# Seven half-block products for the down projections of two feed-forward parts, in an fp32 transformer kernel

## The reference, cut to what matters

```python
def swiglu_ffn(x, w_up, w_down):
    gate, up = jnp.split(x @ w_up, 2, axis=-1)
    return (jax.nn.silu(gate) * up) @ w_down
...
h = h + swiglu_ffn(rmsnorm(h, norm_ffn[l]), ffn_w_up[l], ffn_w_down[l])
```

## Time and profile before

| | |
|---|---|
| time, median of 3 runs | 1587.54 us (1587.21 to 1591.04) |
| span of the profiled execution | 1588.5 us |
| TensorE busy | 1557.8 us, 98% of the span |
| VectorE / ScalarE / GpSimd busy | 66% / 51% / 51% |
| TensorE's granted clock, mean | 0.995 of full speed |

### The profile page before, as it was taken

How to read it: one execution, slowest core, us unless ns; L and a number is a source line. 1 busy time by engine, 2 the same in 40 slices (tenths; PEclk the granted TensorE clock), 3 DMA queues, 4 the chain that set the end, 5 groups by cost and what they waited for, 6 DMA issues and landing times.

```text
span 1588.5 us, 26988 instructions
## 1 busy us (share of the span) xinstructions
PE 1557.8 (98%) x10227; PEld 1356.5 (85%) x10227; DVE 1050.6 (66%) x1622; ACT 816.2 (51%) x1334; POOL 812.8 (51%) x459
## 2 busy tenths in 40 slices
PE   6999999999999999999999999999999999999997
PEld 4888888888887878478998998988788998998996
DVE  6887587597597859977734643664666762572555
ACT  4555455355356535376633542654666652453453
POOL 1444345345345439827655654654116665564653
PEclk8999999999999999999999999999999999999999
DMA  9322322322323365712332332352112333233231
GB/s 376 140 93 80 120 83 91 119 82 90 119 81 102 128 116 153 187 53 81 107 119 80 106 119 81 105 182 96 54 41 68 106 112 100 93 106 115 85 117 69
DMA packets 53640, 172.86 MB, mean 109 GB/s; under 512 B 5403, under 2 KB 11580, under 8 KB 53052
## 3 DMA queue, kind: packets, MB, share of 16 engines
q1 hardware_dynamic: 47296, 159.90, 30.6%
q10 hardware_dynamic: 6268, 11.95, 3.2%
HBM read 165.48 MB, written 6.36 MB: 108 GB/s over the span
## 4 chain that ended last, share of the span: by engine, by line
PE 79%; DVE 3%; issue 2%; ACT 2%; POOL 2%; DVEq 0%; ACTq 0%; POOLq 0%
PE gps L2026 13%; PE gps L2028 12%; PE gps L2027 12%; PE gps L2449 6%; PE gps L2451 6%; PE gps L2450 6%; PE aps L2449 3%; PE aps L2451 3%; PE aps L2450 3%; PE gps L2386 2%; PE gps L2084 1%; PE gps L2086 1%; PE gps L2085 1%; POOL w_lo L619 1%; PE aps L2527 1%
## 5 line engine op out<-in xcount | busy, mean ns | idle before, releaser
L619 POOL TENSOR_TENSOR w_lo<-w_raw,w_hi 128x1024 fp32r<-128x1024 f32 x172 | 437.4, 2547 | 545.9 <-ACT w_hi L741 545.8
L2026 PE MATMUL gps<-xa_hi,w_hi 128*128 128x512 f32 x767 | 306.6, 400 | 2.6 <-DVE xa_lo L1380 2.6
L2027 PE MATMUL gps<-xa_lo,w_hi 128*128 128x512 f32 x767 | 299.9, 391 | 0.0
L2028 PE MATMUL gps<-xa_hi,w_lo 128*128 128x512 f32 x767 | 299.8, 391 | 0.0
L741 ACT CAST w_hi<-w_raw 128x1024 fp32r<-128x1024 f32 x172 | 180.0, 1046 | 155.6 <-PE gps L2028 75.2
L2026 PEld LDWEIGHTS gps<-xa_hi,w_hi 128*128 128x128 f32 x767 | 144.6, 188 | 35.3 <-DVE xa_lo L1380 4.1
L2028 PEld LDWEIGHTS gps<-xa_hi,w_lo 128*128 128x128 f32 x767 | 144.6, 188 | 31.1
L2027 PEld LDWEIGHTS gps<-xa_lo,w_hi 128*128 128x128 f32 x767 | 144.8, 189 | 27.6
L2026 PE MATMUL gps<-xb_hi,w_hi 128*128 128x512 f32 x378 | 148.2, 392 | 0.0
L2028 PE MATMUL gps<-xb_hi,w_lo 128*128 128x512 f32 x378 | 147.2, 389 | 0.0
L2027 PE MATMUL gps<-xb_lo,w_hi 128*128 128x512 f32 x378 | 147.1, 389 | 0.0
(11 more groups left out here) (428 smaller groups left out, 4324.9 us busy)
## 6 DMA issues: line engine op xcount, KB each, us to landing
w_raw<-weights_dram SPq DMA_DIRECT2D x268, 512.0 KB, 3.5
ada_w<-ada_in_dram SPq DMA_DIRECT2D x8, 1024.0 KB, 18.1
gates<-ret_tab_dram ACTq DMA_DIRECT2D x4, 1024.0 KB, 6.0
spread<-glu_scratch_dram SPq DMA_DIRECT2D x12, 270.0 KB, 5.1
rel_scratch_dram<-rel_rows ACTq DMA_DIRECT2D x1, 3072.0 KB, 34.5
x<-x_turned_dram SPq DMA_DIRECT2D x2, 1024.0 KB, 7.2
res<-xT_dram ACTq DMA_DIRECT2D x1, 2048.0 KB, 9.5
bias<-rel_scratch_dram ACTq DMA_DIRECT2D x1, 2048.0 KB, 9.8
```

The costliest lines, as they stand in the source:

```text
L619: TT(w_lo[:, j, :], w_raw[:, j, :], w_hi[:, j, :].bitcast(F32), ALU.subtract).then_inc(lo_ready[j], 1)
L2026: mm(gps[:, j, :], w_hi[:, j, w], x[0][:, k, :], start=k == 0, stop=False)
L2027: mm(gps[:, j, :], w_hi[:, j, w], x[1][:, k, :], start=False, stop=False)
L2028: last = mm(gps[:, j, :], w_lo[:, j, w], x[0][:, k, :], start=False, stop=k == blocks - 1)
```

## The change

The down projections of parts 0 and 1 of each layer become seven-product groups too, in one order with the up groups (`FF_ORDER`, 30 groups a layer: 22 up, 8 down). A down group makes two output chunks from the 8 hidden chunks of its part. Part 2 stays dense. The up group `("up", part + 1, 0)` is run ahead of the down groups of the part before it.

For this the hidden rows have to be mixed as the inputs were: after each odd hidden chunk VectorE makes three differences of 256 columns (a fourth, `t1`, is made after the even chunk), ScalarE casts the four together (`hidden_mix_high`), and VectorE makes their low parts (`hidden_mix_low`). The gated rows now go to SBUF (`hbuf`) rather than back to PSUM. The norm's factor is left off the up rows of these parts and applied to the results of the down groups (`down_added`), which are then added to `res`. TensorE waits for all mixed rows of a part ahead of its first down group. Weights are reordered on the host; their number is the same, 68 chunks a layer.

```diff
 FF_PARTS = (8, 8, 6)
+MIXED_PARTS = 2
...
+def ff_order():
...
+    order, starts = [], [sum(FF_PARTS[:part]) for part in range(len(FF_PARTS))]
+    for part, n in enumerate(FF_PARTS):
+        order += [("up", part, k) for k in range(1 if part else 0, n)]
+        if part < MIXED_PARTS:
+            order += [("up", part + 1, 0)] + [("down", part, m) for m in range(KC // 2)]
+    return order, starts
...
+                def silu(I, s):
                     act.wait_ge(evicted[s], I + 2)
                     nc.scalar.activation(sq[:, s, :], sq[:, s, :], ACT.Silu).then_inc(silu_ready, 1)
...
-                def hidden_high(f, k, s):
-                    act.wait_ge(ff_ready, f + 1)
-                    nc.scalar.copy(halves(hidden[:, k, :]), UP_ROWS[s]).then_inc(ff_hi, 1)
...
+                def hidden_high(f, part, k):
+                    row = hbuf[:, 2 * (k % 2), :]
+                    act.wait_ge(rows_free, f + 3)
+                    if part >= MIXED_PARTS:
+                        ins = nc.scalar.copy(hidden[:, k, :], row)
+                    elif k % 2 == 0:
+                        ins = nc.scalar.copy(hid_single(k // 2)[:, 0, :], row[:, 0:TH])
+                    else:
+                        ins = nc.scalar.copy(hid_double(k // 2)[:, :, 0, :], halves(row))
+                    ins.then_inc(hid_high, 1)
+                def hidden_mix_high(part, m):
+                    act.wait_ge(hid_mixed, mixes_before(layer, part) + m + 1)
+                    nc.scalar.copy(hid_mix(layer, m, 0), hid_rows).then_inc(hid_mix_high, 1)
...
+                for n in range(FF_PAIRS):
...
+                    kind, part, k = FF_ORDER[n - 1] if n else (None, None, None)
+                    early = kind == "up" and k == 0 and part > 0
...
+                    if more:
+                        first_row_high(I1, s1)
...
+                    if kind == "up":
+                        silu(up + (n - 1) // 2, 1 - s)
+                    if n > 1:
+                        first_copy(f, I, s)
+                    if more and n > 0:
+                        sums_high(I1, f + 1, s1)
+                    copied(f, 2, hbuf[:, 2 * s + 1, TH:], UP_SUM[s])
+                    if kind == "up" and not early:
+                        hidden_high(f - 1, part, k)
+                    copied(f, 3, hbuf[:, 2 * s + 1, 0:TH], UP_ROW[s])
...
+                    copied(f, 4, GATE_ROW[s][:, TH:], UP_ROW[s])
+                    if more:
+                        last_sum_high(f + 1, s1)
...
+                    if kind == "down" and k == KC // 2 - 1:
+                        act.wait_ge(tile_done[2 * (1 - s) + 1], up + (n - 1) // 2 + 2)
+                        hidden_high(f0 + FF_ORDER.index(("up", part + 1, 0)), part + 1, 0)
+                    if kind == "up" and part < MIXED_PARTS and k % 2 == 1:
+                        hidden_mix_high(part, k // 2)
...
             def ffn(layer, hidden_hi, hidden_lo, norm, n_next, build=None):
...
+                def gate_and_up(n, part, k):
+                    f, I, s = f0 + n, up + n // 2, n % 2
+                    if n == 0:
                         dve.wait_ge(rstd_ready, norm + 1)
                     dve.wait_ge(tile_done[2 * s + 1], I + 2)
                     TT(sq[:, s, :], GATE_ROW[s], rstd[:], ALU.mult).then_inc(evicted[s], 1)
                     own.done(TT(UP_ROWS[s], UP_ROWS[s], halves(hbuf[:, 2 * s + 1, :]), ALU.add))
-                    own.done(TT(UP_ROWS[s], UP_ROWS[s], halves(rstd[:]), ALU.mult))
-                    dve.wait_ge(silu_ready, f + 1)
-                    TT(UP_ROWS[s], UP_ROWS[s], halves(sq[:, s, :]), ALU.mult).then_inc(ff_ready, 1)
-                def hidden_low(f, k, s):
-                    dve.wait_ge(ff_hi, f + 1)
-                    TT(halves(hidden_lo[:, k, :]), UP_ROWS[s], halves(hidden_hi[:, k, :]).bitcast(F32), ALU.subtract).then_inc(ff_lo, 1)
-                    if s == 1:
-                        for j in (2, 3):
-                            dve.sem_inc(evicted[j], 1)
...
-                    for k in range(n):
-                        f, I, s = f0 + k, up + k // 2, k % 2
-                        if k > 0:
-                            gate_and_up(f - 1, up + (k - 1) // 2, 1 - s)
-                        if part == 0 and k == 0:
-                            dve.wait_ge(sq_used, USED[norm] + KC - 2)
-                        if k + 1 < n:
-                            sums_low(f + 1, 1 - s)
-                            last_sum(f + 1, 1 - s)
-                        if k > 0:
-                            hidden_low(f - 1, k - 1, 1 - s)
-                        if k + 1 < n:
-                            last_sum_low(f + 1, 1 - s)
-                        if k + 2 < n:
-                            two_sums(up + (k + 2) // 2, f + 2, s)
-                    gate_and_up(f, I, s)
-                    hidden_low(f, k, s)
...
+                    if part >= MIXED_PARTS:
+                        own.done(TT(UP_ROWS[s], UP_ROWS[s], halves(rstd[:]), ALU.mult))
+                    dve.wait_ge(silu_ready, hidden_at(layer, part, k) + 1)
+                    TT(halves(hbuf[:, 2 * s, :]), UP_ROWS[s], halves(sq[:, s, :]), ALU.mult).then_inc(rows_free, 1)
+                    rows_taken(s)
...
+                def down_added(n, m):
+                    I, s = up + n // 2, n % 2
+                    dve.wait_ge(tile_done[2 * s + 1], I + 2)
+                    summed = own.mark(TT(UP_ROWS[s], UP_ROWS[s], halves(hbuf[:, 2 * s + 1, :]), ALU.add))
+                    first = own.mark(TT(sq[:, s, :], GATE_ROW[s], rstd[:], ALU.mult))
+                    dve.sem_inc(evicted[s], 1)
+                    own.wait(summed)
+                    second = own.mark(TT(UP_ROWS[s], UP_ROWS[s], halves(rstd[:]), ALU.mult))
+                    own.wait(first)
+                    TT(res[:, 2 * m, :], sq[:, s, :], res[:, 2 * m, :], ALU.add)
+                    own.wait(second)
+                    TT(halves(res[:, 2 * m + 1, :]), UP_ROWS[s], halves(res[:, 2 * m + 1, :]), ALU.add).then_inc(rows_free, 1)
+                    rows_taken(s)
...
+                def hidden_low(part, k):
...
+                    even, odd = hbuf[:, 0, :], hbuf[:, 2, :]
+                    row, m = (even, odd)[k % 2], k // 2
+                    dve.wait_ge(hid_high, hidden_at(layer, part, k) + 1)
+                    if part >= MIXED_PARTS:
+                        TT(hidden_lo[:, k, :], row, hidden_hi[:, k, :].bitcast(F32), ALU.subtract).then_inc(hid_low, 1)
+                    elif k % 2 == 0:
+                        one = hid_single(m)
+                        TT(one[:, 1, :], row[:, 0:TH], one[:, 0, :].bitcast(F32), ALU.subtract).then_inc(hid_low, 1)
+                        dve.wait_ge(hid_low, hidden_at(layer, part, k) + 1)
+                        made["t1"] = own.mark(TT(even[:, 0:TH], even[:, TH:], even[:, 0:TH], ALU.subtract))
+                    else:
+                        two = hid_double(m)
+                        own.wait(made["t1"])
+                        own.mark(TT(even[:, TH:], odd[:, TH:], even[:, TH:], ALU.subtract))
+                        TT(two[:, :, 1, :], halves(row), two[:, :, 0, :].bitcast(F32), ALU.subtract).then_inc(hid_low, 1)
+                        dve.wait_ge(hid_low, hidden_at(layer, part, k) + 1)
+                        own.done(TT(odd[:, TH:], odd[:, TH:], even[:, 0:TH], ALU.subtract))
+                        TT(odd[:, 0:TH], odd[:, 0:TH], odd[:, TH:], ALU.subtract).then_inc(hid_mixed, 1)
+                def hidden_mix_low(part, m):
+                    dve.wait_ge(hid_mix_high, mixes_before(layer, part) + m + 1)
+                    TT(hid_mix(layer, m, 1), hid_rows, hid_mix(layer, m, 0).bitcast(F32), ALU.subtract).then_inc(hid_mix_low, 1)
...
+                for n in range(FF_PAIRS):
...
+                    kind, part, k = FF_ORDER[n - 1] if n else (None, None, None)
+                    early = kind == "up" and k == 0 and part > 0
+                    if kind == "up":
+                        gate_and_up(n - 1, part, k)
+                    if kind == "down":
+                        down_added(n - 1, k)
...
+                    if n + 1 < FF_PAIRS:
+                        sums_low(f + 1, 1 - s)
+                        last_sum(f + 1, 1 - s)
+                    if kind == "up" and not early:
+                        hidden_low(part, k)
+                    if n + 1 < FF_PAIRS:
+                        last_sum_low(f + 1, 1 - s)
+                    if n + 2 < FF_PAIRS:
+                        two_sums(up + (n + 2) // 2, f + 2, s)
+                    if kind == "down" and k == KC // 2 - 1:
+                        hidden_low(part + 1, 0)
+                    if kind == "up" and part < MIXED_PARTS and k % 2 == 1:
+                        hidden_mix_low(part, k // 2)
...
-                    ready_k = lambda k: pe.wait_ge(ff_lo, f0 + k + 3)
-                    if part < len(FF_PARTS) - 1:
-                        with pe.Fori(0, KC // SLOTS) as i:
```

(59 more changed lines are left out.)

222 lines of the change are left out of this document (98 added, 124 removed).

## The result

The changed kernel takes 1607.75 us (median, 1606.34 to 1610.85) against 1587.53 us before; the ratio is 1.0121 (95% interval 1.0109 to 1.0133). It is slower by 20 us; 1604.7 was forecast. The profiled span is 1609.1 us (before 1588.5).

The account below looks back on a forecast made before the run. TensorE's stream was taken as the bound. Stalls of 15.4 + 10.4 + 3.4 + 0.8 = 30.0 us less 12.8 gained gave +17.2 us, so 1604.7 us; range 1583 to 1615, the forecast's own 1599 to 1611.

Parts of the forecast that it names:

- the gain of 12.8 us: TensorE: 16 pairs of output chunks go from 10.88 to 10.08 us each, 12.8 us gained.
- The chain of the gate row: Mixed low part delays gate row, silu and copy; TensorE's third product stalls 1.3 us in 12 groups, 15.4 us.
- 1.13 to the next start: VectorE's added 1024-column operation: 1.21 us long, the next operation starting 1.13 us after it starts.
- The port: Mixed low part, reading two SBUF tiles, arrives at G + 10.47, waits for GpSimd until G + 11.5, ends at G + 12.5.
- the third rival: VectorE: a difference loses two turns to GpSimd, 12 groups stall 2.3 us instead of 1.3; 1617 us, chance 0.14.
- It is hidden: Last difference on VectorE ends at worst at G + 8.0, when ScalarE is about to be free for the mixed cast.
- the first rival: No port wait at the mixed low part, VectorE needing a 0.3 us lead: 12.8 us of stalls, 1587 us, chance 0.17.
- The first down groups: TensorE waits ahead of them for a part's last mixed low part, 2.6 us late, four times: 10.4 us.
- The rows left over: VectorE's rows after the down groups: 1.7 us late twice after part 0's, 0.4 twice after part 1's; 3.4 plus 0.8.
- The rival of no change: Mixed low part does not wait for the port; stalls of 12.8 us cancel the gain, 1587 us, chance 0.17.

Follow-up runs that it names:

- The best version: Changed kernel with mixed low part behind the gate row except a part's last, TensorE's wait behind product w11, left-over rows at the ordinary place: 1586.73 us, 0.9964 of kernel before.

## Why the prediction was right

**The bound and the gain.** Down groups in the changed kernel start 10.08 us apart, as forecast from the earlier trace rows; the gain of 12.8 us is real. The formula for a lone matmul on the page of the Trainium skill "TensorE: Matmul & The Clock Gate" (Back-to-back issue gap) would have made it 19, an estimate; no run here shows such distances. The best version bears the 12.8 out: its stalls with their restarts are 4 x 1.06 + 2 x 0.67 + 2 x 0.36 = 6.3 us, which would leave 6.5, and 6.0 were measured (3.5 to 8.0 by the interval).

**The chain of the gate row.** 12 stalls as placed, 1.27 to 1.51 us from start to start, 1.15 to 1.39 of it lost and 0.10 more at the first matmul: 16.9 us against 15.4. The run with the low part behind the gate row shows that the place makes them. One number of the working is not in its row: "1.13 to the next start" of a 1024-column operation, where the earlier trace rows have 1.24 (the next operation there waits for its result). The changed kernel bears out what was meant: the gate row starts 0.08 us ahead of the low part's end (787.00 against 787.08).

**The port.** Forecast: the low part starts 0.2 us behind GpSimd and ends about 1 us late. Measured 2.14 us in seven of 16 groups and 2.11 in four, the last of each part. In the other five groups it took 1.21, without a wait, and TensorE stalled as long (1.27 to 1.51 us). These are the first odd chunk of each part and once the second:

```profile
759.39 1.40 DVE L1989 TENSOR_TENSOR hbuf<-hbuf 128x256 f32<-128x256 f32 x1
760.82 1.40 DVE L1990 TENSOR_TENSOR hbuf<-hbuf 128x256 f32<-128x256 f32 x1
...
764.30 1.22 DVE L1995 TENSOR_TENSOR xa_mix<-hbuf,xa_mix 128x1024 fp32r<-128x1024 f32 x1
```

```profile
764.32 2.33 POOL L733 TENSOR_TENSOR w_lo<-w_raw,w_hi 128x512 fp32r<-128x512 f32 x1 [2.38 <-ACT w_hi L1080]
```

Here both differences lost a turn, which is how the third rival begins, and the mixed cast waited for them. So the line "It is hidden" of the prediction fails in these groups. All that follows came later; VectorE was now 0.02 us ahead of GpSimd, which is the condition of the first rival, and it was GpSimd that waited (2.33 us). That the stall came out at the same size is luck: the prediction did not have this path. The page "SBUF — State Buffer" of the Trainium skill (Who interferes with whom) has VectorE contend with GpSimd when it reads two SBUF inputs and not with one; the run with the PSUM input agrees, 1.22 against 2.14 us.

**The first down groups.** 2.72 and 2.71 us from start to start, so 2.6 us late and not quite 0.1 more at the restart, 2.6 forecast in all. Right within 0.1, four times.

**The rows left over.** 1.51 us twice (1.7 forecast) and 0.48 twice (0.4). Right in order and size; the run with these rows at the ordinary place took most of them away.

**What was not in the sum.** One stall of 0.68 us, and the granted clock at half after two of the four waits of 2.4 us, together some 3.6 us. 16.9 + 10.7 + 3.0 + 0.9 + 3.6 = 35.1 us of stalls less 12.8 is 22.3; the groups of the two layers take 11.1 and 10.5 us more than before (323.6 and 322.6 against 312.4 and 312.1), 21.6 together. The spans differ by 20.6, since the feed-forward begins 1.1 us earlier in this execution. So the stalls were put 5 us too low, and 2.9 of the 5 are the clock, which the forecast did not price behind waits of this length.

The rival of no change (no wait for the port at the mixed low part) is refuted twice: 11 of 16 low parts waited, and with that wait taken away the ratio is still 1.0060. What keeps it there are the waits of the differences and the 3.9 us of the left-over rows, which the rival's sum had at 0.3.

## What to carry to other kernels

Where one engine's stream has no gaps, price an added operation on another engine by its place in the hand-written order: find the result that the busy engine waits for next, and the slack of the chain that leads to it. Here 1.2 us of work and 0.9 us of waiting, ahead of a chain with 0.8 us of slack, cost 1.4 us each time; just behind the chain's first link they cost that chain nothing, and 0.9 us at each of the four places that wait for the work itself. Two engines that take turns at a port make the cost of moving an operation hard to foresee: casting the next weight row earlier shortened one wait where there was one, and made two where there was none.
